# Both heads of a pair at once in grouped-query and neighbourhood attention

## The chip, the cores and the metric

The kernel runs on one core of a Trainium2 chip. The metric is the device time of one execution in microseconds; of several runs the median is given. A core has TensorE (PE in the profile; its weight loads stand apart as PEld), VectorE (DVE), ScalarE (ACT), GpSimd (POOL) and SyncE (SP), each with its own instruction queue, worked through in order. They meet at semaphores. Matmul results go to PSUM, eight banks of 128 partitions by 512 f32; all else is in SBUF.

## The reference

Two models in series on 512 tokens of width 1024. The first has a recurrent mixer, a feed-forward layer, stick-breaking attention with 16 heads and a second feed-forward layer. The change lies in the second model, whose core is:

```python
def second_block(x, mem, w_in, b_gate, na_rpb, gqa_q_gain, gqa_k_gain, w_mem_kv, w_branch, ...):
    z = jnp.einsum('bsd,df->bsf', x, w_in[l])
    q_na, k_na, v_na, q_g, k_g, v_g, q_m, gate_logits = jnp.split(z, _split_points(), axis=-1)
    y_na = neighbourhood_attention(...)      # 8 heads of 64
...
    y_gqa = gqa_attention(...)               # 8 query heads of 64, 2 key heads
...
    y_mem = memory_attention(...)            # 4 heads of 128
    branches = jnp.stack([y_na, y_gqa, y_mem], axis=2)
    proj = jnp.einsum('bsgk,gkd->bsgd', branches, w_branch[l])
    gates = jax.nn.sigmoid(gate_logits + b_gate[l]).reshape(B, S, N_BRANCH, D)
    merged = jnp.sum(gates * proj, axis=2)
    mix = jnp.einsum('bsd,de->bse', merged, w_out[l])
    x = layer_norm(DN_ALPHA * x + mix, ln1_g[l], ln1_b[l])
    ffn = expert_choice_ffn(x, w_router[l], w_gate_up[l], w_down[l])
    return layer_norm(DN_ALPHA * x + ffn, ln2_g[l], ln2_b[l])

def gqa_attention(...):                      # q, k: rms_norm, then rope
    s = jnp.einsum('bkgqd,bskd->bkgqs', qi, k) * scale
    p = jax.nn.softmax(s, axis=-1)
    return jnp.einsum('bkgqs,bskd->bqkgd', p, v)

def neighbourhood_attention(...):            # 8 rows x 64 columns; 4 blocks of 16 query columns
    scores = jnp.einsum('rcqhd,rckwhd->hrcqkw', qg, k_blk) * (1.0 / math.sqrt(dh))
    scores = jnp.where(in_win, scores + bias, NEG_INF)
    p = jax.nn.softmax(scores, axis=(-2, -1))
    out = jnp.einsum('hrcqkw,rckwhd->rcqhd', p, v_blk)
```

In grouped-query attention four query heads share one key head. In neighbourhood attention a query sees all 8 rows and 16 columns; `bias` comes from a table with 15 x 31 entries for each head, and entries outside the window are masked.

## The kernel before

Activations are held transposed: features on partitions, the 512 tokens along the free axis. A dense product in f32 is made of three matmuls (lines 1604 to 1606): high half by high half, low by high, high by low. `HH`/`HL` (and `YP` for attention outputs) are the halves of the activations, `WH`/`WL` those of the weights. SP loads weights into six `RAW` buffers; ACT makes `WH` (L958) and DVE `WL` (L1206), in three buffers each. A "unit" of weights is up to eight 128 x 128 tiles, and a "triple" the three matmuls of one tile.

**Order.** `Order` writes the program as a list of steps. `claim` takes the PSUM bank that was released longest ago, and notes the event after which it may be written; `release` gives it back with that event. Every engine's program walks the same list and issues its part of each step, so the order of the list is the order on each engine. The second mixer has banks 0 to 5 for this ring and banks 6 and 7 for attention outputs. Its order is written by hand in `mixer2_order`.

**Weave.** `staged` goes over the units of an attention. Per unit it adds the score step, then takes pieces of other work from the generator `work` (the "fill"; `counts` says how many pieces), then adds the value step that has become due, then the turn of the unit two places back. A piece is four triples: twelve matmuls. "Turn" is the transposing of a probability tile: PE multiplies it by the identity (L1647) into a bank, ACT copies it to SBUF (L969).

**Grouped-query stage.** Heads are treated in four pairs `c`. The two heads of a pair lie on partitions 0 to 63 and 64 to 127 of `ZG` (queries) and `KG` (keys, both key heads), which are views of the tile `AT`. A unit is one head and 128 queries: 32 units. Its score is one matmul with 64 contracted rows (L1782). DVE takes the maximum from the bank (L1225) and scales it (L1227), ACT makes the exponential and its sum (L964) into one of three `PG`, DVE takes the reciprocal (L1232) and scales `PG` (L1234), PE turns it, and ACT copies into `GT2`. When a head's four units are turned, its values are made by four matmuls over 512 columns (L1797). The fill is the gates and branch products of the memory attention (group 2), and the queries of pairs 1 to 3 with norm and rope: one product in plain f32 for the norm, one for the rotation (L1775), a reciprocal over 512 columns (L1432). The program lists f32 matmuls as two passes (`x2` in the timeline for one instruction).

**First neighbourhood pair.** After the last values, `finish(pairs[0]["qkv"]())` projects the queries, keys and values of pair 0 with nothing woven in.

**Neighbourhood stage.** A unit is one head and one block of 16 query columns in all 8 rows: 128 queries, 32 units. `nq` stores the queries ordered by column block. The score matmul has 256 keys, the band of 32 columns in 8 rows (L1807). The bias is added by a second matmul into the same bank (L1811): `anti`, a matrix that reverses the order of partitions, times a window of `BI`. `BI` holds the table's rows as POOL's queue loads them (L909, 16 small DMAs for a pair); in that layout the queries run backwards. DVE adds the mask and takes the maximum in one instruction into `SN`; ACT makes the exponential into `PN`, DVE scales, PE turns (two transposes), ACT copies into `NT`, and two matmuls over 128 columns make the values (L1828). The fill is the projection of pairs 1 to 3 and the gates and branches of the grouped-query output (group 1); their gate products are added up by POOL (L913).

## Time and profile before

| | us |
|---|---|
| median of 3 runs | 2364.69 (2362.87 to 2369.45) |
| the profiled execution | 2363.75 |
| its span in the trace | 2362.0 |
| busy in the span: PE, DVE | 2197.8 (93%), 1113.5 (47%) |
| busy in the span: ACT, POOL | 720.3 (30%), 156.4 (7%) |

The memory attention and all that goes before it end at 1302.76 in the trace, when the first grouped-query score begins. The grouped-query stage lasts until 1466.29; its last fill matmul begins at 1420.08. The first neighbourhood pair is projected until 1485.50, and the last neighbourhood values begin at 1674.44. Behind them come the group-0 branches, the output product, a layer norm, the router and the experts. In a timeline equal instructions in a row are one line with `xN`, and its second number is from the start of the first to the end of the last; matmuls overlap, so that the next line can begin before this one ends.

### The profile page before, as it was taken

What the parts mean: (1) busy time and instruction counts of PE and PEld (TensorE: products, weight loads), DVE (VectorE), ACT (ScalarE), POOL (GpSimd) and SP (SyncE); (2) the same over time, 40 slices, a digit from 0 to 9 for tenths busy, and PEclk for the clock granted to TensorE, in tenths of its full rate; (3) what the DMA queues carried; (4) which work ended last, traced back from release to release, by engine and by line L of the source; (5) the groups of instructions that cost most, each with busy time, mean ns of one, the idle gap of its engine ahead of it and who ended that gap; (6) DMA issues with size and microseconds to landing.
All of it is one profiled execution on the core that took longest, in us unless ns stands there. A gap on an engine that the chain in (4) does not pass through costs nothing.

```text
span 2362.0 us, 24184 instructions
## 1 busy us (share of the span) xinstructions
PE 2197.8 (93%) x9722; PEld 1523.0 (64%) x9722; DVE 1113.5 (47%) x1602; ACT 720.3 (30%) x1051; POOL 156.4 (7%) x159
## 2 busy tenths in 40 slices
PE   6989999999999899999989998999995899999995
PEld 4768888888777788888877554777783433334331
DVE  7876443445665654344566554444455211111114
ACT  2553322333555432222344443233333000000002
POOL 2221000001000100000100001210002000000001
PEclk9989999999999999999999999999998899999997
DMA  4222223223111222332341111321226799999992
GB/s 160 89 71 99 96 75 124 90 74 123 63 56 61 81 90 85 112 99 80 108 134 49 50 50 33 76 56 54 81 72 249 282 371 406 410 409 411 410 418 85
DMA packets 83662, 350.74 MB, mean 148 GB/s; under 512 B 9152, under 2 KB 10832, under 8 KB 66912
## 3 DMA queue, kind: packets, MB, share of 16 engines
q1 hardware_dynamic: 80448, 342.92, 39.5%
q0 software_dynamic: 2240, 2.71, 0.8%
q10 hardware_dynamic: 864, 3.57, 0.4%
q8 instruction: 78, 1.28, 0.2%
q14 instruction: 32, 0.26, 0.0%
HBM read 347.06 MB, written 2.10 MB: 148 GB/s over the span
## 4 chain that ended last, share of the span: by engine, by line
PE 85%; DVE 8%; ACT 3%; issue 3%; POOL 0%; DMA 0%; ACTq 0%; DVEq 0%; POOLq 0%
PE PS L1604 19%; PE PS L1606 18%; PE PS L1605 18%; PE PS L1904 10%; PE PS L1935 5%; PE PS L1947 2%; PE PS L1647 2%; PE PS L1887 2%; PE PS L1797 1%; PE PS L1782 1%; PE PS L1811 1%; PE PS L1807 1%; PE PS L1703 1%; PE PS L1828 1%; PE PS L1717 1%
## 5 line engine op out<-in xcount | busy, mean ns | idle before, releaser
L1604 PE MATMUL PS<-HH,WH 128*128 128x512 f32 x1392 | 564.8, 406 | 33.7 <-DVE HL L1210 20.7
L1606 PE MATMUL PS<-HH,WL 128*128 128x512 f32 x1392 | 547.3, 393 | 0.0
L1605 PE MATMUL PS<-HL,WH 128*128 128x512 f32 x1392 | 547.0, 393 | 0.0
L1206 DVE TENSOR_TENSOR WL<-RAW,WH 128x1024 fp32r<-128x1024 f32 (+5 forms) x300 | 339.7, 1132 | 245.0 <-ACT WH L958 243.7
L958 ACT ACTIVATE WH<-RAW 128x1024 fp32r<-128x1024 f32 (+4 forms) x278 | 263.3, 948 | 311.3 <-PE PS L1606 311.3
L1604 PEld LDWEIGHTS PS<-HH,WH 128*128 128x128 f32 x1392 | 264.3, 190 | 107.4 <-issue 28.1
L1606 PEld LDWEIGHTS PS<-HH,WL 128*128 128x128 f32 x1392 | 264.2, 190 | 57.0
L1605 PEld LDWEIGHTS PS<-HL,WH 128*128 128x128 f32 x1392 | 264.9, 190 | 55.2 <-issue 2.4
L1904 PE MATMUL PS<-SL,XS 128*64 128x512 f32 x952 | 227.2, 595 | 0.0
L1313 DVE TENSOR_TENSOR X<-X,PS 128x512 f32<-128x512 f32 x116 | 79.6, 686 | 228.4 <-PE PS L1947 162.2
L1904 PEld LDWEIGHTS PS<-SL,XS 128*64 128x64 f32 x952 | 70.1, 137 | 133.8 <-issue 126.8
L1604 PE MATMUL PS<-MH,WH 128*128 128x512 f32 x352 | 136.9, 389 | 0.0
L1605 PE MATMUL PS<-ML,WH 128*128 128x512 f32 x352 | 136.9, 389 | 0.0
L1606 PE MATMUL PS<-MH,WL 128*128 128x512 f32 x352 | 136.9, 389 | 0.0
L1935 PE MATMUL PS<-SL,HT 128*64 128x512 f32 x480 | 113.3, 602 | 5.5 <-ACT HT L969 5.5
L1180 ACT ACTIVATE SG<-PS 128x512 f32<-128x512 f32 x16 | 8.7, 594 | 328.7 <-PE PS L1904 328.7
L1935 PEld LDWEIGHTS PS<-SL,HT 128*64 128x64 f32 x480 | 36.3, 138 | 77.3 <-issue 69.8
L1216 DVE TENSOR_TENSOR U<-PS,RS 128x512 f32<-128x512 f32 x44 | 30.4, 691 | 107.2 <-PE PS L1606 107.2
L1606 PEld LDWEIGHTS PS<-MH,WL 128*128 128x128 f32 x352 | 66.1, 188 | 13.8
L1604 PEld LDWEIGHTS PS<-MH,WH 128*128 128x128 f32 x352 | 66.1, 188 | 13.7
L1605 PEld LDWEIGHTS PS<-ML,WH 128*128 128x128 f32 x352 | 66.1, 188 | 13.6
L1579 DVE TENSOR_TENSOR SG<-SG,PS 128x512 f32<-128x512 f32 x16 | 10.3, 684 | 132.3 <-ACT SG L1180 132.3
(281 smaller groups left out, 2744.4 us busy)
## 6 DMA issues: line engine op xcount, KB each, us to landing
SL<-in_wgu_dram SPq DMA_DIRECT2D x119, 1024.0 KB, 11.7
SL<-in_wdn_dram SPq DMA_DIRECT2D x60, 1024.0 KB, 9.7
RAW<-in_w_dram SPq DMA_DIRECT2D x46, 512.0 KB, 3.3
RAW<-in_wg_dram SPq DMA_DIRECT2D x44, 512.0 KB, 3.3
RAW<-in_wu_dram SPq DMA_DIRECT2D x44, 512.0 KB, 3.3
RAW<-in_wd_dram SPq DMA_DIRECT2D x32, 384.0 KB, 3.1
RAW<-in_wqkv_dram SPq DMA_DIRECT2D x24, 512.0 KB, 3.3
RAW<-in_wd_dram SPq DMA_DIRECT2D x32, 320.0 KB, 2.9
```

What stands on the lines that cost most here:

```text
L958: e.activation(WH[u % NSPL][:, 0:n], RAW[u % NRAW][:, 0:n], ACT.Copy).then_inc(*whs.did("u", u))
L1206: e.tensor_tensor(wl, raw, wh.bitcast(F), ALU.subtract).then_inc(*wlo.did("u", u))
L1216: e.tensor_tensor(dst, src, r, ALU.mult).then_inc(*scaled.did(*event))
L1313: e.tensor_tensor(X[:, c, :], X[:, c, :], bank(*key), ALU.add).then_inc(*xup.did(*key))
L1604: e.matmul(out, wh[:, w], xh, start=k == 0, stop=False)
L1605: e.matmul(out, wh[:, w], xl, start=False, stop=False)
L1606: m = e.matmul(out, wl[:, w], xh, start=False, stop=k == g.total - 1)
L1647: m = e.transpose(bank(*key)[:, 128 * j:128 * j + 128], src, ident)
L1887: m = e.matmul(bank("ga", q, d)[:, 0:256], P[:, tc, 128 * d:128 * d + 128], PE[:, tc, :], start=tc == 0 and P is XNH, stop=tc == 3 and P i ...
L1904: m = e.matmul(bank("h", i, n)[64 * e2:64 * e2 + 64, :], XS[z][:, k, x0:x0 + 64], SL[(l0 + e2) % NSLOT][:, 512 * n:512 * n + 512], start=k ...
L1935: m = e.matmul(bank("y", i, n)[64 * e2:64 * e2 + 64, :], HT[:, 2 * k + f, 64 * e2:64 * e2 + 64], SL[(l0 + e2) % NSLOT][:, 1024 * f + 512 * ...
L1947: e.matmul(bank("sc", i, d), SG[:, 128 * d:128 * d + 128], GT[i % 2][:, :], start=True, stop=True).then_inc(*ex.did("sc", i, d))
```

## The change

- **Units of two heads.** In both stages a unit is now a pair of heads and 128 queries: 16 units each. The scores of the two heads are issued one behind the other on array rows 0 to 63 and 64 to 127, into a bank each. The values are issued in turns on array columns 0 to 63 and 64 to 127. In the grouped-query stage they are made after every unit, 128 columns wide, in place of once per head, 512 wide. `PG` and `GT2` have four buffers.
- **Softmax.** Two maxima, one small scaling, two exponentials, one small reciprocal, two scalings. The turn of a unit is eight transposes (four in the neighbourhood stage) and two copies by ACT (one).
- **Bias.** The bias matmul goes. POOL adds bias and mask of both heads into `BM` in a new step `na_mask`, 16 in all; the queries are written backwards (`by_column`) so that they fit `BI`, and the outputs are read backwards again. The mask constant is reversed once, at the start of the mixer, by two plain f32 matmuls with `anti` of 512 and 256 columns and two copies by DVE. DVE adds the scores to `BM` in place and takes the maximum.
- **Weave.** The turn comes one unit behind the score, not two. Pieces of fill are two triples, six matmuls; `counts` is [4, 3] and [5]. Pair 0's projection is part of the grouped-query fill. The banks of a unit's two scores come free with its exponentials (with DVE's pass in the neighbourhood stage).

The core of the diff, with its new line numbers in the order further down (1604 has become 1674, 1606 1676, 1647 1717, 1782 1860, 1797 1878, 1807 1888, 1828 1906):

```diff
 def mixer2_order(o):
+    o.claim("mask")
+    o.claim("mask2")
     o.add("m2_consts")
+    for n in range(2):
+        o.release((("mask",), ("mask2",))[n], "gated", "mask", n)
...
+    def staged(groups, work, counts, lag=2):
         units = [(g, u) for g in groups for u in range(g["n"])]
         then = None
-        for i in range(len(units) + 2):
+        for i in range(len(units) + lag):
             if i < len(units):
                 g, u = units[i]
                 while u == 0 and not g["there"]():
...
             if then:
                 then()
             then = None
-            if i >= 2:
-                g, u = units[i - 2]
-                then = g["turn"](u, (i - 2) % 3)
+            if i >= lag:
+                g, u = units[i - lag]
+                then = g["turn"](u, (i - lag) % 3)
+        if then and lag == 1:
+            step(work)
+            then()
+            then = None
...
+            for y in range(2):
+                o.claim("gs", c, u, y)
+            o.add("gqa_score", c, u)
+            for y in range(2):
+                o.release(("gs", c, u, y), "prob", "gs", c, u, y)
         def turn(u, k):
-            key = ("gt2", c, u)
-            o.claim(*key)
-            o.add("gqa_turn", c, u, k)
-            o.release(key, "turn", *key)
+            for y in range(2):
+                o.claim("gt2", c, u, y)
+            o.add("gqa_turn", c, u)
+            for y in range(2):
+                o.release(("gt2", c, u, y), "turn", "gt2", c, u, y)
             def values():
-                if u // 4 == 0:
+                if u == 0:
                     claim_out("go", c)
-                o.add("gqa_values", c, u // 4)
-                if u // 4 == 1:
+                o.add("gqa_values", c, u)
+                if u == 3:
                     release_out(("go", c), "lo", "b", 4 + c)
-            return values if u % 4 == 3 else None
-
-        return {"n": 8, "there": lambda: f"q{c}" in there, "score": score, "turn": turn}
-
...
-    staged([gqa_pair(c) for c in range(4)], gqa_work(), [1])
+            return values
+
+        return {"n": 4, "there": lambda: f"q{c}" in there, "score": score, "turn": turn}
...
+                yield from o.lin_steps((name, c), [("w2", (4 * i + c,), 8)], "h", done, size=2)
+                if i == 1 and c == 0:
+                    o.add("na_bias", 0)
+                    o.add("na_mask", 0, 0)
+            yield
+            for j in range(2):
+                natural(("nvn", c, j))
             there.add(("na", c))
...
+            o.add("na_turn", c, u)
+            o.release(("nt", c, u), "turn", "nt", c, u)
+            if c < 3:
+                o.add("na_mask", c + 1, u)
+            if (c, u) == (0, 3):
+                o.add("na_bias", 3)
...
+    na_pairs = [na_pair(c) for c in range(4)]
+
+    def gqa_work():
+        br = branches(2, 2)
         for c in range(1, 4):
-            q = pairs[c]["qkv"]()
-            for w in "qqbbbqqqqq":
-                step(q if w == "q" else br, 1)
+            q = rope(f"q{c}", 12 + c, 2)
+            for w in "qqqqbbqbbbbqbb" if c == 1 else "qqqqbbqbbbbqbbbbbb":
+                step(q if w == "q" else br)
                 yield
         yield from br
-
-    o.add("na_start")
-    finish(pairs[0]["qkv"]())
-    staged(pairs, na_work(), [1, 2, 1])
+        yield from na_pairs[0]["qkv"]()
+
+    def na_work():
+        br = branches(1, 2)
+        for c in range(1, 4):
+            q = na_pairs[c]["qkv"]()
+            for w in "qqqqqqqqqqqqbbbbqqbbbbbbbb":
+                step(q if w == "q" else br)
+                yield
+        yield from br
+
+    staged([gqa_pair(c) for c in range(4)], gqa_work(), [4, 3], 1)
+    o.add("na_bias", 1)
+    for u in range(1, 4):
+        o.add("na_mask", 0, u)
+    o.add("na_bias", 2)
+    staged(na_pairs, na_work(), [5], 1)
...
-        PG = [sb(f"PG{i}", [128, T], F, pg) for i in range(3)]
-        GT2 = [sb(f"GT2{i}", [128, 4, T], F, pg) for i in range(2)]
+        PG = [sb(f"PG{i}", [128, T], F, pg) for i in range(4)]
+        GT2 = [sb(f"GT2{i}", [128, 4, 128], F, pg) for i in range(4)]
...
+        NT = [t[:, :].rearrange("p (j n) -> p j n", n=128) for t in (ST, SA)]
...
+        def by_column(t):
+            return t.rearrange("p (c n) -> p c n", c=4)[:, :, ::-1].rearrange("p c (r i) -> p r c i", i=16)
...
+                elif kind == "na_mask":
+                    c, cb = a
+                    f = BAND[cb] - 16 * cb + 16
+                    if c:
+                        e.wait_ge(*tr("nt", c - 1, cb))
+                    elif cb == 1:
+                        e.wait_ge(*att("go", 3, 3))
+                    if cb == 0:
+                        e.wait_ge(*gated("mask", 1))
+                        e.wait_ge(*d_bias[c % 2](c, 1, 7))
+                    m = cst("mask", 256 * (0, 1, 1, 2)[cb], 256).rearrange("p (a w) -> p a w", a=8)
+                    e.tensor_tensor(BM[cb][:, :, :].rearrange("p y (a w) -> p y a w", a=8),
+                                    BI[c % 2][:, :, :].rearrange("p y (a w) -> p y a w", a=8)[:, :, :, f:f + 32],
+                                    m.unsqueeze(1).to_broadcast([128, 2, 8, 32]), ALU.add).then_inc(
+                        *pool.did("bm", c, cb))
...
-                    dve_softmax_max(e, key, bank(*key), k, 0.125)
-                    dve_softmax_div(e, key, PG[k][:, :], k)
+                    c, u = a
+                    k = 8 * (u % 2)
+                    for y in range(2):
+                        if y == 0:
+                            e.wait_ge(*att("gs", c, u))
+                        e.tensor_reduce(SM[:, k + y:k + y + 1], bank("gs", c, u, y), AX.X, ALU.max).then_inc(
+                            *masked.did("gs", c, u, y))
+                    e.wait_ge(*masked("gs", c, u, 1))
+                    e.tensor_scalar(SM[:, k + 2:k + 4], SM[:, k:k + 2], -0.125, None, ALU.mult).then_inc(
+                        *smax.did("m", "gs", c, u))
+                    e.wait_ge(*prob("gs", c, u, 1))
+                    e.reciprocal(SM[:, k + 6:k + 8], SM[:, k + 4:k + 6]).then_inc(*smax.did("r", "gs", c, u))
+                    e.wait_ge(*smax("r", "gs", c, u))
+                    for y in range(2):
+                        P = PG[2 * (u % 2) + y][:, :]
+                        e.tensor_scalar(P, P, SM[:, k + 6 + y:k + 7 + y], None, ALU.mult).then_inc(
+                            *smax.did("p", "gs", c, u, y))
...
-                    e.tensor_tensor_reduce(SN[k][:, :], bank(*key)[:, 0:256], cst("mask", 256 * (0, 1, 1, 2)[u % 4], 256),
-                                           1.0, -3e38, ALU.add, ALU.max, SM[:, 4 * k:4 * k + 1]).then_inc(*masked.did(*key))
-                    dve_softmax_max(e, key, None, k, 1.0)
-                    dve_softmax_div(e, key, PN[k][:, :], k)
+                    c, u = a
+                    k = 8 * (u % 2)
+                    e.wait_ge(*att("ns", c, u))
+                    e.wait_ge(*pool("bm", c, u))
+                    for y in range(2):
+                        S2 = BM[u][:, y, :]
+                        e.tensor_tensor_reduce(S2, bank("ns", c, u, y)[:, 0:256], S2, 1.0, -3e38, ALU.add, ALU.max,
+                                               SM[:, k + y:k + y + 1]).then_inc(*masked.did("ns", c, u, y))
...
+                elif kind == "m2_consts":
+                    for n, (a0, w) in enumerate(((0, 512), (512, 256))):
+                        if o.before[(("mask",), ("mask2",))[n]]:
+                            e.wait_ge(*freed(("mask", "mask2")[n]))
+                        e.matmul(bank(("mask", "mask2")[n])[:, 0:w], anti, cst("mask", a0, w), start=True,
+                                 stop=True).then_inc(*red.did("mask", n))
...
-                    e.matmul(bank("gs", c, u), ZG[c % 2][p:p + 64, 128 * qc:128 * qc + 128], KG[p:p + 64, :], start=True,
-                             stop=True).then_inc(*att.did("gs", c, u))
+                    for y in range(2):
+                        p = 64 * y
+                        m = e.matmul(bank("gs", c, u, y), ZG[c % 2][p:p + 64, 128 * u:128 * u + 128], KG[p:p + 64, :],
+                                     start=True, stop=True)
+                    m.then_inc(*att.did("gs", c, u))
...
+                    e.wait_ge(*turn("gt2", c, u, 1))
                     for j in range(4):
-                        m = e.matmul(bank("go", c)[p:p + 64, :], VG[:, 128 * j + p:128 * j + p + 64], GT2[y][:, j, :],
-                                     start=j == 0, stop=j == 3)
-                    m.then_inc(*att.did("go", c, y))
+                        for y in range(2):
+                            p = 64 * y
+                            m = e.matmul(bank("go", c)[p:p + 64, 128 * u:128 * u + 128], VG[:, 128 * j + p:128 * j + p + 64],
+                                         GT2[2 * (u % 2) + y][:, j, :], start=j == 0, stop=j == 3, skip_group_check=True)
+                    m.then_inc(*att.did("go", c, u))
...
-                    e.matmul(out, NQ[c % 2][p:p + 64, 0, 128 * cb:128 * cb + 128],
-                             NQ[c % 2][p:p + 64, 1, :].rearrange("p (r w) -> p r w", r=8)[:, :, bs:bs + 32], start=True,
-                             stop=False)
-                    e.wait_ge(*d_bias[c % 2](c, 1, 7))
-                    e.matmul(out, anti, BI[c % 2][:, y, :].rearrange("p (a w) -> p a w", a=8)[:, :, f:f + 32], start=False,
-                             stop=True).then_inc(*att.did("ns", c, u))
+                    for y in range(2):
+                        p = 64 * y
+                        m = e.matmul(bank("ns", c, u, y)[:, 0:256], NQ[c % 2][p:p + 64, 0, 128 * u:128 * u + 128],
+                                     window(u, NQ[c % 2][p:p + 64, 1, :]), start=True, stop=True)
+                    m.then_inc(*att.did("ns", c, u))
```

TensorE in the first half of the grouped-query stage, from the end of one run of fill to the next. The kernel before:

```order
L1606 MATMUL PS<-HH,WL 128x512
L1797 MATMUL PS<-GT,AT 64x512 x4
L1647 MATMUL PS<-C,PG 128x128 x4
L1782 MATMUL PS<-AT 128x512
L1604 MATMUL PS<-HH,WH 128x512
```

The changed kernel, the same place:

```order
L1676 MATMUL PS<-HH,WL 128x512
L1878 MATMUL PS<-GT,AT 64x128 x8
L1717 MATMUL PS<-C,PG 128x128 x8
L1860 MATMUL PS<-AT 128x512 x2
L1674 MATMUL PS<-HH,WH 128x512
```

One head's four value matmuls over 512 columns, which came once in four units, have become eight over 128 columns in every unit, and the one score two.

TensorE in the neighbourhood stage, a unit between two runs of fill. The kernel before:

```order
L1606 MATMUL PS<-HH,WL 128x512
L1828 MATMUL PS<-NT,NV 64x128 x2
L1647 MATMUL PS<-C,PN 128x128 x2
L1807 MATMUL PS<-AT 128x256
L1811 MATMUL PS<-BI,C 128x256
L1604 MATMUL PS<-HH,WH 128x512
```

The changed kernel:

```order
L1676 MATMUL PS<-HH,WL 128x512
L1906 MATMUL PS<-ST,NV 64x128 x4
L1717 MATMUL PS<-C,BM 128x128 x4
L1888 MATMUL PS<-AT 128x256 x2
L1674 MATMUL PS<-HH,WH 128x512
```

The matmul with `BI` is gone, and the rest stands twice in a unit, of which there are half as many.

DVE in the grouped-query stage, one softmax and the fill behind it. The kernel before:

```order
L1225 TENSOR_REDUCE SM<-PS 128x1
L1227 TENSOR_SCALAR SM<-SM 128x1
L1232 RECIPROCAL SM<-SM 128x1
L1234 TENSOR_SCALAR PG<-PG,SM 128x512
L1432 RECIPROCAL ST<-ST 128x512
L1434 SCALAR_TENSOR_TENSOR AT<-AT,V,ST 128x512
L1206 TENSOR_TENSOR WL<-RAW,WH 128x512
L1403 SCALAR_TENSOR_TENSOR ACC<-ACC,PS 128x512
```

The changed kernel:

```order
L1504 TENSOR_REDUCE SM<-PS 128x1 x2
L1507 TENSOR_SCALAR SM<-SM 128x2
L1510 RECIPROCAL SM<-SM 128x2
L1514 TENSOR_SCALAR PG<-PG,SM 128x512 x2
L1256 TENSOR_TENSOR WL<-RAW,WH 128x512
L1456 SCALAR_TENSOR_TENSOR ACC<-ACC,PS 128x512
L1485 RECIPROCAL ST<-ST 128x512
L1487 SCALAR_TENSOR_TENSOR AT<-AT,V,ST 128x512
```

The chain of both heads stands in one block ahead of the fill's work, and the rope's long reciprocal one place further on.

## Rows read from the trace of the kernel before

**Rows 1.** The page, chain of work that ended last: shares of the span by engine.
```profile
PE 85%; DVE 8%; ACT 3%; issue 3%; POOL 0%; DMA 0%; ACTq 0%; DVEq 0%; POOLq 0%
```
**Rows 2.** Windows view: us, busy (instructions) by engine, PEclk, DMA share, GB/s.
```profile
1302.76:1466.29 163.53, 154.00 (x534) 83.43 (x533) 90.29 (x177) 69.58 (x131) 0.00 (x0) 0.97 0.13 42
1466.29:1485.50 19.21, 17.61 (x81) 14.29 (x81) 7.50 (x11) 3.67 (x4) 16.71 (x32) 1.00 0.61 109
1485.50:1674.44 188.94, 188.41 (x850) 135.71 (x849) 86.41 (x230) 58.33 (x132) 27.79 (x40) 1.00 0.21 60
```
**Rows 3.** Timeline of PE, grouped-query stage: start, duration, instruction, [idle before <-releaser].
```profile
1352.85 1.12 PE L1782 MATMUL PS<-AT 64*128 64x512 f32 x2
1353.90 0.50 PE L1604 MATMUL PS<-YP,WH 128*128 128x512 f32 x1
...
1356.86 3.65 PE L1797 MATMUL PS<-GT,AT 128*64 128x512 f32 x8
1360.44 0.66 PE L1647 MATMUL PS<-C,PG 128*128 128x128 f32 x4
```
**Rows 4.** Timeline of PE, neighbourhood stage, one unit and the fill behind it.
```profile
1527.89 0.65 PE L1828 MATMUL PS<-NT,NV 128*64 128x128 f32 x4
1528.47 0.44 PE L1647 MATMUL PS<-C,PN 128*128 128x128 f32 x2
1528.84 0.70 PE L1807 MATMUL PS<-AT 64*128 64x256 f32 x2
1529.47 0.70 PE L1811 MATMUL PS<-BI,C 128*128 128x256 f32 x2
1529.82 0.58 PE L1604 MATMUL PS<-HH,WH 128*128 128x512 f32 x1
1530.24 0.39 PE L1605 MATMUL PS<-HL,WH 128*128 128x512 f32 x1
...
1532.53 0.39 PE L1606 MATMUL PS<-HH,WL 128*128 128x512 f32 x1
1532.85 0.32 PE L1828 MATMUL PS<-NT,NV 128*64 128x128 f32 x1
```
**Rows 5.** PE's groups by form; the last row is of 1466.29 to 1674.43.
```profile
L1797 PE MATMUL PS<-GT,AT 128*64 128x512 f32 x64 | 34.0, 681 | 7.0 <-ACT GT L969 7.0
L1604 PE MATMUL PS<-HH,WH 128*128 128x512 f32 x56 | 24.1, 430 | 0.0
...
L1604 PE MATMUL PS<-HH,WH 128*128 128x512 f32 x160 | 67.5, 422 | 0.0
```
**Rows 6.** Timeline of PE near the end of the grouped-query stage.
```profile
1436.09 5.34 PE L1797 MATMUL PS<-GT,AT 128*64 128x512 f32 x8 [2.16 <-ACT GT L969]
```
**Rows 7.** Timeline of PE in the first model's attention, two heads at once.
```profile
762.77 2.43 PE L1703 MATMUL PS<-QK 64*128 64x384 f32 x16
...
765.68 2.37 PE L1727 MATMUL PS<-WT,VN 128*64 128x512 f32 x16
```
**Rows 8.** Timeline of DVE in the bare end of the grouped-query stage.
```profile
1431.43 0.68 DVE L1225 TENSOR_REDUCE SM<-PS 128x1 f32<-128x512 f32 x1
1432.15 0.15 DVE L1227 TENSOR_SCALAR SM<-SM 128x1 f32<-128x1 f32 x1
1433.21 0.16 DVE L1232 RECIPROCAL SM<-SM 128x1 f32<-128x1 f32 x1 [0.91 <-ACT PG L964]
1433.41 0.48 DVE L1234 TENSOR_SCALAR PG<-PG,SM 128x512 f32<-128x512 f32 x1
```
**Rows 9.** DVE's groups by form in the grouped-query stage.
```profile
L1432 DVE RECIPROCAL ST<-ST 128x512 f32<-128x512 f32 x3 | 10.1, 3353 | 3.9 <-ACT ST L1101 3.9
```
**Rows 10.** Timeline of POOL in the neighbourhood stage.
```profile
1524.61 8.33 POOL L909 DMA_DIRECT2D BI<-in_rpb_dram  x16 [17.30 <-PE PS L1811]
1547.19 1.28 POOL L913 TENSOR_TENSOR ACC<-ACC,GX 128x512 f32<-128x512 f32 x1 [14.25 <-DVE GX L1403]
```
**Rows 11.** Timeline of PE at the start of the second mixer.
```profile
1201.92 0.55 PE L1604 MATMUL PS<-YP,WH 128*128 128x256 f32 x1 [5.14 <-DVE YP L1210]
```

247 lines of the change are left out of this document (117 added, 130 removed).

## The prediction

> **What bounds the kernel now.** I read the chain of waits first: TensorE makes up 85% of it [rows 1]. A saving therefore counts only if it takes away TensorE's time or its idling. I then split the second mixer into stretches [rows 2]. From the first grouped-query score at 1302.76 us to the last neighbourhood value matmul at 1674.44 us there are 371.7 us: 163.5 for the grouped-query stage, 19.2 in which the first neighbourhood pair is projected with nothing else running, and 188.9 for the neighbourhood stage. DVE is busy for 90.3, 7.5 and 86.4 us of them, so no other engine is the limit there yet.
>
> Durations of single matmuls mislead, since they overlap; I price by the distance from one start to the next. The dense matmuls that are woven in (the "fill") start 0.229 us apart (ten steps from 1530.24 to 1532.53), and a run of 12 takes 3.03 us in the neighbourhood stage and 2.96 in the grouped-query stage (1353.90 to 1356.86), so a run costs 0.28 and 0.21 on top of its 12 x 0.229 [rows 3, 4]. One head's score, with 64 contracted rows, takes 1.05, a head's four value matmuls over 512 columns 3.58 for eight passes (1356.86 to 1360.44), 0.43 a pass [rows 3]. In the neighbourhood stage one head's quarter costs values 0.58, two transposes 0.37, score 0.63, bias 0.35, together 1.93, and there are 32 [rows 4]. A narrow pass (128 columns) more costs (0.58 - 0.37) / 2, about 0.11.
>
> The end of the grouped-query stage differs. Its fill is used up at 1420, and the last 10 scores and 13 turns run bare. The value groups wait 7.0 us in all for ACT's copies [rows 5], and the one at 1436.09 takes 5.34 us behind its wait, where 3.65 is usual [rows 3, 6]; two later ones do the same. The granted clock over the stage is 0.97, against 1.00 in the stretches behind it [rows 2]: after these pauses the engine ran for a while at the lower of its two levels, 1.2 instead of 2.4 GHz. Waits and slow passes are worth some 7.0 + 3 x 1.6 = 12 us.
>
> **The change, part by part.** The fill itself doesn't change: 56 + 32 triples in the first stretch and 160 + 32 in the rest [rows 5]; the 32 are the branch matmuls, as the code has them, 840 matmuls in all; the new order has 336 + 504. I price the new stretch afresh and compare it with 371.7.
>
> *Both heads at once.* Do two halves of the array overlap? The first model's attention already issues its heads so. L1703 has 1280 columns of scores per head, for two heads, in two passes; L1727 the same number of value columns, on column halves. At 0.43 us per 512-column pass, one head alone would take 2560 / 512 x 0.43 = 2.15, two in turn 4.3. Measured are 2.43 and 2.37 [rows 7]: they overlap nearly fully, on row halves and on column halves. So a pair's score costs 1.05 as one head's did: 16 x 1.05 = 16.8. A unit's values are eight matmuls over 128 columns; four such passes take 0.58, so eight overlapped steps take 0.58 + 4 x 0.11 = 1.02: 16.3. Eight transposes behind values take 0.37 + 6 x 0.11, 1.02: 16.3. The six rope matmuls have two passes of 0.43: 5.2. Together 54.6.
>
> *Neighbourhood stage.* The bias matmul is gone. A unit now has values 0.58 (four overlapped steps), four transposes 0.59, and a score pair of 0.35 (as L1811, which stood last before fill): 1.52, 16 times 24.3, and 4 x 8 x 0.11 = 3.5 for the NB transposes: 27.8.
>
> *Fill.* 840 x 0.229 = 192.4; 18 runs x 0.21 and 19 x 0.28 add 9.1, where 22 and 34 runs added 14.1. Together 201.5.
>
> Sum: 201.5 + 54.6 + 27.8 = 283.9 without waits.
>
> *Waits that take their place.* A unit's score now needs banks that the exponentials of the unit before it read, so there is a loop: score, two maxima, two exponentials, next score. In the bare stretch one head's chain on DVE is 0.72 from the maximum's start to the next step, 1.06 to the reciprocal, 0.20 to the scaling and 0.48 for that [rows 8]; the other head adds a maximum (0.68), an exponential (about 0.8, what the 1.06 holds besides the 0.15 step and the hops) and a scaling (0.4, overlapped): 4.3 us, in which DVE stands still for ACT. From score to next score the loop needs 0.1 + 0.72 + 0.68 + 1.06 + 0.8 + 1.1 = 4.5, and TensorE has work for 5.5 to 8.8 between them. What matters is DVE's backlog. Over the first twelve units DVE has 12 x 4.3 = 51.6 plus fill work: 34 operations over 512 columns at 0.68, 6 over 1024 at twice that and 3 reciprocals of 3.35 [rows 8, 9], 41.4, in all 93.0. TensorE has 93.9 (228 fill matmuls 52.2, entries 2.5, ropes 5.2, 12 scores 12.6, 11 turns 11.2, 10 value groups 10.2). They are level. One place walked through: behind unit 2's chain DVE has four pieces of fill, and behind unit 1's the rope's reciprocal, so unit 3's maxima start about 3.3 us after its score; its interval of 6.8 us (12 fill matmuls, rope, values, turn, score) is then 1.0 short. There are three such places: 3 us. At the end of the stage the last values wait for two copies right behind the turn: 0.9. At the end of the neighbourhood stage two value groups wait for a copy each: 1.5. 1.0 for everything else. Together 6.4; bounds 0 and 25 (first rival).
>
> *Moved to POOL.* 16 adds of bias and mask, at 1.27 each as L913 over the same size [rows 10], take the place of the bias matmuls. Only the first pair is tight: behind the last grouped-query values POOL issues 16 DMAs (8.33) and then adds, so BM1 is ready 9.7 us later; its score comes after 1.0 + 0.35 + 7.2, DVE then waits about 1 us, and two runs of fill (14 us) lie before the transposes that need it. With that cover gone it would cost 1 us. Four adds and 16 issues in a pair, 13.4 us, lie beside 37 us of TensorE.
>
> *Mask reversal.* Two f32 matmuls of 512 and 256 columns at the start of the mixer, two passes each, 0.86 + 0.43 and 0.2 for entering. The chain to ScalarE, the reciprocal and the YP split, for which TensorE waits 5.14 us [rows 11], starts behind them. So they cost 1.5 in full; the two DVE copies fall into a time in which DVE waits for that chain.
>
> **Result.** 283.9 + 6.4 = 290.3 against 371.7 is -81.4; with +1.5, -79.9. The profiled execution took 2363.75 us (span 2362.0), so 2283.9; the runs' median is 0.9 above it: **2285 us**. What follows (last branches, experts) is the same in both orders and only moves earlier.
>
> **The rivals.**
> - *DVE becomes the bound of the grouped-query stage* (0.22). For it: 93.0 against 93.9 us leave nothing for hops or late gates. Against: the last four units have slack, and back to back operations start closer than their durations. If each of 16 units loses 1 to 1.3 us more: +16 to +21, 2301 to 2306. The Trainium skill (TensorEngine Tiling (Array Packing), PSUM Bottleneck) warns that packing speeds up TensorE but not the emptying of PSUM, which may become the limit; by that rule the time would be this rival's.
> - *The halves don't overlap in narrow passes* (0.08), or the change doesn't do what it says. Weight loads come four times as often per column as in the widest part of L1727. Values would cost 16 x 0.87 + 16 x 0.44 = 21 more: 2306; scores too, 13.8 + 6.9 more: 2327. Against: L1727's narrow part is inside its 2.37.
> - *No new waits, and the mask reversal hidden* (0.12): 2277.
> - *Slower than before* (0.02): POOL's adds read a broadcast mask and windows of the bias tile, a form that no row shows. A pair leaves POOL 37 us, of which 8.3 go to issues and 3.4 to the gate adds; above 6.4 us an add, POOL sets the pace. To lose 87 us over the 12 adds of the last three pairs each would need 13.7 us, eleven times its row: 2372 and more.
>
> **Chances.** Forecast (2280 to 2292) 0.55, the rivals as above, 0.01 for anything else. The range 2273 to 2306 holds the forecast, the case without waits and most of the DVE case. About 0.3% (7 us) is what a measurement of this kernel can tell from no change; all but the last rival lie far beyond: faster 0.97, same 0.01, slower 0.02.
>
> **What would show it.** Matmuls of L1860 and of L1878 starting in pairs, 1.05 us a score pair and 1.02 a value group. A granted clock of 1.00 over the whole stretch. TensorE waiting about 1 us ahead of L1860 at three places, not at sixteen. The stretch at 290 us. POOL's adds at 1.3 us, and DVE waiting for them once. The forecast is wrong if score pairs take 2 us, if TensorE waits ahead of most scores, or if stretches outside this one move by more than 2 us.

## The result and the profile after

The changed kernel takes 2297.84 us in the median of 4 runs (2295.93 to 2298.65), the kernel before 2364.44; the ratio is 0.9714, with a 95% interval of 0.9697 to 0.9730. The forecast was 2285. It is faster by 66.6 us, 12.8 less than forecast. That is inside the range of 2273 to 2306, above the forecast's own band (2280 to 2292, chance 0.55), and below the band of the first rival (2301 to 2306). The profiled execution took 2297.08 us, its span is 2295.3.

The page of the changed kernel, shares of its chain by engine (before: [rows 1]):

```profile
PE 82%; DVE 10%; ACT 4%; issue 3%; POOL 0%; DMA 0%; ACTq 0%; DVEq 0%; POOLq 0%
```

The two stages of the changed kernel in the windows view (columns as in [rows 2]): from the first grouped-query score to the first neighbourhood score, with the projection of neighbourhood pair 0 inside, and from there to the end of the last values.

```profile
1306.19:1455.12 148.93, 138.59 (x805) 97.56 (x805) 90.23 (x155) 71.54 (x135) 10.33 (x19) 0.99 0.21 58
1455.12:1606.30 151.18, 149.69 (x786) 114.12 (x785) 81.94 (x199) 55.56 (x116) 60.38 (x70) 1.00 0.31 78
```

Together 300.1 us stand against the 371.7 of [rows 2]: -71.6. In the second stage TensorE is busy for all but 1.5 us. In the first it isn't: 10.3 us are idle. TensorE's waits in that stage, by what ended them (us in total, times, longest):

```profile
PE PS L1860 <- DVE AT L1497: 5.2, 3, 3.4
PE PS L1674 <- DVE ACC L1456: 2.8, 3, 1.3
PE PS L1845 <- ACT SQ L1140: 1.2, 1, 1.2
PE PS L1878 <- ACT GT L1012: 0.8, 1, 0.8
PE PS L1851 <- DVE ACC L1456: 0.4, 1, 0.4
```

L1860 is the score, L1497 VectorE's last step of the rope of a pair's queries, L1456 VectorE's addition of a branch product, whose bank the fill wants next. TensorE's timeline in that stage, one unit (against [rows 3]):

```profile
1359.99 1.09 PE L1878 MATMUL PS<-GT,AT 128*64 128x128 f32 x16
1361.01 1.09 PE L1717 MATMUL PS<-C,PG 128*128 128x128 f32 x8
1362.04 1.13 PE L1860 MATMUL PS<-AT 64*128 64x512 f32 x4
1363.10 1.12 PE L1851 MATMUL PS<-AT,C 128*128 128x512 f32 x2
1365.50 0.47 PE L1674 MATMUL PS<-HH,WH 128*128 128x512 f32 x1 [1.28 <-DVE ACC L1456]
```

From start to start the values of both heads take 1.02 us, their eight transposes 1.03, both scores 1.06: within 0.01 of the forecast's 1.02, 1.02 and 1.05. The halves overlap: the first passes of the two heads start 0.01 us apart in both groups. The last row is one of the waits. The timeline of a neighbourhood unit (against [rows 4]):

```profile
1584.03 0.66 PE L1906 MATMUL PS<-SA,NV 128*64 128x128 f32 x8
1584.62 0.66 PE L1717 MATMUL PS<-C,BM 128*128 128x128 f32 x4
1585.20 0.70 PE L1888 MATMUL PS<-AT 64*128 64x256 f32 x4
1585.83 0.50 PE L1674 MATMUL PS<-HH,WH 128*128 128x512 f32 x1
```

Values 0.59 and turn 0.58 are as forecast; the score pair takes 0.63, where 0.35 was put. The longest pause, where the rotation of pair 3's queries stands right ahead of that pair's first score:

```profile
1406.11 1.02 PE L1851 MATMUL PS<-AT,C 128*128 128x512 f32 x2
1410.56 1.82 PE L1860 MATMUL PS<-AT 64*128 64x512 f32 x4 [3.43 <-DVE AT L1497]
1412.32 0.79 PE L1674 MATMUL PS<-HH,WH 128*128 128x512 f32 x1
1412.91 0.63 PE L1675 MATMUL PS<-HL,WH 128*128 128x512 f32 x1
```

Behind 3.43 us of idleness the score pair takes 1.76 us from start to start, where 1.06 is usual, and a fill matmul 0.43 (1412.91 to the next at 1413.34), where 0.23 is. These are passes at the lower clock level (1.2 GHz where 2.4 is usual; the granted clock is the third number from the end of the row, 0.54), 1.6 us in all with the run of fill behind the score (6.58 for 24 matmuls against 5.66):

```profile
1410.56:1414.19 3.63, 3.63 (x8) 1.79 (x9) 1.46 (x3) 0.23 (x1) 0.00 (x0) 0.54 0.01 2
```

### The profile page after: what moved, and what is told of

It reads as the page before. It is cut to its first block, busy times and chain, and to the rows that moved or that the text cites. A ratio compares the mean times of both kernels' runs of the same rounds, so it can differ in the third digit from the quotient of the medians.

```text
span 2295.3 us, 24304 instructions
## 1 busy us (share of the span) xinstructions
PE 2132.7 (93%) x9854; PEld 1506.7 (66%) x9854; DVE 1102.7 (48%) x1540; ACT 715.8 (31%) x1035; POOL 182.7 (8%) x175
## 4 chain that ended last, share of the span: by engine, by line
PE 82%; DVE 10%; ACT 4%; issue 3%; POOL 0%; DMA 0%; ACTq 0%; DVEq 0%; POOLq 0%
PE PS L1674 19%; PE PS L1676 18%; PE PS L1675 18%; PE PS L1982 10%; PE PS L2013 5%; PE PS L2025 2%; PE PS L1965 2%; PE PS L1717 2%; PE PS L1779 1%; DVE XC L1322 1%; PE PS L1793 1%; PE PS L1803 1%; DVE X L1565 1%; PE PS L1860 1%; DVE WL L1256 1%
## 5 line engine op out<-in xcount | busy, mean ns | idle before, releaser
L1649 DVE TENSOR_TENSOR SG<-SG,PS 128x512 f32<-128x512 f32 x16 | 10.3, 683 | 132.3 <-ACT SG L1230 132.3
```

## The experiments

Each is an edit of the changed kernel, run once (the last two four times), and is judged by its stage lengths in the trace. "The stage" is the grouped-query stage, from the first grouped-query score to the first neighbourhood score: 148.9 us in the changed kernel. Stage lengths are finer than the whole time, since identical code scatters outside the edited stages, above all ahead of the mixer: from the first matmul to the mixer's norm the changed kernel and the nine edits with the same code there take 1176.3 to 1182.3 us. Stage lengths scatter too, but only by the clock. Of the three edits that leave the grouped-query stage as it is, two have 148.9 us and one 150.2, with the same waits (10.3 us) and with passes at the lower clock for 5.9 us behind the wait of 3.42 where the changed kernel has 3.6. So a difference of 1.3 us in that stage can be the clock alone. The neighbourhood stage has 151.2 us in every run that leaves it as it is. Three theories stood against each other for the 12 us lost in the grouped-query stage: the place of the rope (1), VectorE's load (2), and a few tight places where both meet (3).

**Rope of pair 3 earlier.**

```diff
-            for w in "qqqqbbqbbbbqbb" if c == 1 else "qqqqbbqbbbbqbbbbbb":
+            for w in "qqqqbbqbbbbqbb" if c < 3 else "qqqqbbqbbbbqbbbbbb":
```

> One edit to the changed kernel: four branch pieces behind the queries of pair 2 are moved behind those of pair 3, so that the last rotation of pair 3 stands two pieces of fill ahead of pair 3's first score, as it does for pairs 1 and 2, and not right ahead of it. Theory 1 (the waits come from where the rope stands): the wait of 3.43 us ahead of that score becomes about 0.9 as at pairs 1 and 2, and the slow passes behind it (0.7 at the score, 0.9 at the fill) go: stage 148.9 us becomes about 144.8, time about 2293.7. Theory 2 (VectorE's whole load sets the pace): the wait only changes its place, under 1 us is gained, 2297.

Measured 2302.06 us; the stage became longer, 154.0 us. The 3.43 us went, and another wait came in its place. ScalarE's timeline there:

```profile
1378.55 0.20 ACT L1153 ACTIVATION_READ_ACCUMULATOR PG<-PS,SM 128x1 f32 x1
1387.59 1.06 ACT L1001 ACTIVATE WH<-RAW 128x1024 fp32r<-128x1024 f32 x1 [8.84 <-PE PS L1676]
1390.54 0.63 ACT L1140 ACTIVATE SQ<-AT 128x512 f32<-128x512 f32 x1 [1.89 <-DVE AT L1266]
1391.08 1.06 ACT L1012 ACTIVATE GT<-PS 128x512 f32<-128x512 f32 x2
```

ScalarE stood 8.84 us at a weight split. The queries of pair 3 now began in the middle of a gate's unit of weights; the split wants the buffer of that unit, which TensorE only gave back after the queries. The rope's square, the copies and the exponentials were queued behind it, and TensorE waited 3.8 us for the square. Neither theory 1 nor theory 2 had this wait. At the stage's end, 3.2 us came from fill that was left over: one piece more behind the last values, and a wait of 1.6 for the neighbourhood values.

**Softmax split on VectorE.**

```diff
             if i < len(units):
...
                 g["score"](u, i % 3)
-            step(work, counts[i % len(counts)])
+            n = counts[i % len(counts)]
+            if i < len(units) and "div" in g:
+                step(work)
+                n -= 1
+                units[i][0]["div"](units[i][1])
+            step(work, n)
...
                 elif kind == "gqa_score":
...
+                elif kind == "gqa_div":
+                    c, u = a
+                    k = 8 * (u % 2)
                     e.wait_ge(*prob("gs", c, u, 1))
```

> One edit to the changed kernel: on VectorE the reciprocal and the two scalings of a unit stand behind the first piece of fill after its score, not straight behind the maxima, in both stages; in the changed kernel VectorE stands still for 1.51 us there in each of 16 units, waiting for ScalarE's exponentials (24.2 us in the grouped-query stage). Theory 2 (VectorE's load with its standing is the limit): the fill's waits for banks of branch products (2.8 + 0.4 us), and two of the three waits for roped queries (0.87, 0.89) go; the third (3.43) shrinks by 1.5: -5 to -6, time about 2292. Theory 1 (place of the rope alone): the waits for roped queries shrink by under 1 us each, time 2296 to 2297.

Measured 2302.65 us, of which 4.1 more than in the changed kernel lie among the experts, in code that the edit doesn't touch. The stage: 147.6 us, -1.4. TensorE's waits there fell by 2.5 us: those ahead of the first scores of pairs 1 and 2 went, as theory 2 had it, but the third is still 3.0, and the fill's waits for banks of branch products grew (4.0 us, from 3.2). Passes at the lower clock took about 1.2 us more than in the changed kernel. The neighbourhood stage, where the edit applies too, has 151.2 us as before. VectorE's waits in the grouped-query stage show why so little was gained:

```profile
DVE WL L1263 <- ACT WH L1008: 23.9, 13, 2.5
...
DVE SM L1520 <- ACT PG L1160: 8.2, 6, 1.5
```

In the changed kernel the second wait is 24.2 us, 16 times, and the first 7.6. Much of the wait has only changed its name: the weight split that VectorE now reaches needs ScalarE's half, which stands behind the same exponentials on ScalarE.

**Mask reversed in the table of constants.**

```diff
-        c[:, CST["mask"] + 256 * n:CST["mask"] + 256 * n + 256] = np.where(m, 0.0, -1e30)
+        c[:, CST["mask"] + 256 * n:CST["mask"] + 256 * n + 256] = np.where(m, 0.0, -1e30)[::-1]
```

with the two matmuls, the two copies and POOL's wait on them taken out.

> One edit to the changed kernel: the mask stands reversed in the table of constants, and the two matmuls and two VectorE copies that reverse it at the start of the second mixer go. Measured between the two traces, TensorE is 1.3 us later there. If that is the whole price: the norm's first matmul comes 1.3 us sooner, time 2296.5. If the reversal also cost the 0.9 us by which the memory attention starts later still: 2295.6. If it was hidden (a rival of the prediction): no change, 2297.8.

Measured 2292.86 us, 4.2 less than the changed kernel's profiled execution, 3.8 of it ahead of the mixer's norm, where the scatter is larger than the mask's price. So whole times don't give that price; the changed kernel's trace does, from the start of the first row to that of the second:

```profile
1186.06 1.45 PE L1756 MATMUL PS<-C 128*128 128x512 f32 x4
1187.16 0.58 PE L1674 MATMUL PS<-HH,WH 128*128 128x512 f32 x1
```

1.1 us, and 0.19 for the next matmul's late start behind it (0.42 against 0.23): 1.3. The wait for the norm's split is 5.1 us with and without the reversal, so nothing hid it. The 0.9 us by which the memory attention started later are 0.7 less in five of the nine experiments that have the reversal: most of them come and go, and aren't its price.

**Projection of neighbourhood pair 0 outside the weave.**

```diff
-        yield from na_pairs[0]["qkv"]()
...
+    finish(na_pairs[0]["qkv"]())
     o.add("na_bias", 1)
```

> One part of the change undone: the projection of neighbourhood pair 0 is no part of the grouped-query fill, but runs with nothing woven in behind that stage, as before. The fill is then 240 matmuls and is used up after about ten of sixteen units. If the weave carries gain: each of the six bare units has 3.1 us of TensorE's work in a loop of at least 4.5, about +8; the bare projection waits 1.6 as before, and slow passes come behind the waits, 1 to 4: +11 to +14, time 2309 to 2312. If the gain comes from the overlap of the heads alone: +0 to +3, up to 2301.

Measured 2298.83 us. The stage, with the bare projection in it, has 153.4, +4.5. The mechanism was right and the count wrong: the fill lasts for 14 of the 16 units, not ten. Only two scores stand bare. The end of the stage, with the value groups waiting for copies:

```profile
1428.61 1.13 PE L1860 MATMUL PS<-AT 64*128 64x512 f32 x4
1430.91 1.09 PE L1878 MATMUL PS<-GT,AT 128*64 128x128 f32 x16 [1.17 <-ACT GT L1012]
1431.93 1.09 PE L1717 MATMUL PS<-C,PG 128*128 128x128 f32 x8
1434.90 1.09 PE L1878 MATMUL PS<-GT,AT 128*64 128x128 f32 x16 [1.88 <-ACT GT L1012]
```

So the new place of this projection is worth 4.5 of the 71.6 us.

**Rope earlier, unit of weights whole.**

```diff
-            for w in "qqqqbbqbbbbqbb" if c == 1 else "qqqqbbqbbbbqbbbbbb":
+            for w in ("qqqqbbqbbbbqbb", "qqqqbbqbbbbq", "qqqqbbqbbbbqbbbbbb")[c - 1]:
```

> The edit of the first experiment again, but the queries of pair 3 now start at the end of a whole branch product (six pieces moved, not four). In the first experiment they started in the middle of a gate's unit of weights; ScalarE's next split then waited 8.8 us for a weight buffer, with the rope's square and the exponentials queued behind it. Theory 3 (place of the rope, if no unit of weights is left half used): the wait of 3.43 us and the slow passes behind it go, about 0.9 is left, and the wait for a weight buffer is under 2: stage (first grouped-query score to first neighbourhood score) 148.9 becomes 144.5 to 145.5. Theory 2 (VectorE's load): the stage gains under 1 us, 148 or more.

Measured 2293.77 us, but the stage has 148.9 us as before. ScalarE's wait for a weight buffer fell to 2.1 and the 3.43 went. Not all pausing did: the last score of pair 2 now starts after 1.74 us of idleness, for which the profile names no cause, and passes at the lower clock stand behind it (granted clock 0.58 and 0.50 in the next two stretches of 1.8 us):

```profile
1397.03 1.85 PE L1860 MATMUL PS<-AT 64*128 64x512 f32 x4 [1.74 <-issue]
```

Up to the last values 3.2 us were gained, and the same 3.2 lost at the end, by the fill that is left over as in the first experiment. A gain and a loss of different causes: this run alone can't decide for theory 3.

**Maxima taken twice, and a short reciprocal.**

```diff
+                        e.tensor_reduce(SM[:, 16 + k // 2 + y:17 + k // 2 + y], bank("gs", c, u, y), AX.X, ALU.max)
                         e.tensor_reduce(SM[:, k + y:k + y + 1], bank("gs", c, u, y), AX.X, ALU.max).then_inc(
                             *masked.did("gs", c, u, y))
```

> The changed kernel with VectorE's two maxima of every grouped-query unit taken twice (the extra result goes to an unused place): 1.2 us more of VectorE in each of 16 units, 19 in all. Theory 2 (VectorE's load sets this stage's pace, the prediction's first rival): +13 to +19, stage 162 to 168. Theory 3 (only the seven places at which rope or branch work meets a softmax are tight): each of them grows by up to 1.2, the rest is hidden: +5 to +8, stage 154 to 157.

```diff
-                    e.reciprocal(ST[:, :], ST[:, :]).then_inc(*roped.did("r", name))
+                    w = 512 if name in ("k", "q0") else 8
+                    e.reciprocal(ST[:, 0:w], ST[:, 0:w]).then_inc(*roped.did("r", name))
```

> The changed kernel with the rope's reciprocal of the queries of pairs 1 to 3 done over 8 columns and not 512, so that these queries are scaled otherwise than in the reference: VectorE has 3.25 us less at each of three places. Theory 3: the maxima behind it start sooner, the wait for pair 3's queries goes from 3.43 to about 0.2 to 1, the 0.70 and 1.28 us waits of the fill and the 0.87 and 0.89 at pairs 1 and 2 shrink: -4 to -7, stage 142 to 145. If the chain over ScalarE and TensorE is what takes the time and not VectorE's queue: under -1.

Measured 2302.21 and 2287.92 us. The stage in the windows view, first with the maxima twice, then with the short reciprocal (VectorE's busy time is the third in the row, 109.18 and 81.24):

```profile
1301.05:1461.78 160.73, 141.00 (x805) 99.04 (x804) 109.18 (x187) 70.89 (x135) 10.55 (x19) 0.97 0.18 54
```

```profile
1301.50:1445.27 143.77, 138.08 (x805) 98.22 (x804) 81.24 (x155) 71.90 (x135) 10.44 (x19) 0.99 0.21 60
```

With 19.0 us more on VectorE the stage is 11.8 longer, with 9.0 less it is 5.2 shorter: 0.6 us for each. Theory 2 wanted 13 or more and theory 3 at most 8; it lies between. TensorE's waits become 19.6 and 5.7 us (10.4 in the changed kernel), for the most part at the same places; with the maxima twice a wait of 1.45 ahead of another score comes in, one that waits for exponentials. In waits alone it is 9.2 more and 4.7 less, 0.5 us for each microsecond of VectorE. VectorE is no full bound and has no slack either: it is busy for 90.2 us, stands 24.2 for the exponentials and 7.6 for weight splits, 122 of 149.

**Values head by head.**

```diff
-                    for j in range(4):
-                        for y in range(2):
+                    for y in range(2):
+                        for j in range(4):
```

> The changed kernel with the eight grouped-query value matmuls of a unit issued head by head (four of one head, then four of the other), not in turns. If the two column halves overlap only because neighbours in the queue lie on different halves: a unit's values take 0.58 + 12 x 0.11 = 1.9 us, not 1.03, 16 x 0.87 = +14, stage 163. If the order doesn't matter (what is saved is saved by the narrower write alone): values stay at 1.03, no change.

Measured 2297.49 us. The value group in TensorE's timeline:

```profile
1323.36 1.58 PE L1878 MATMUL PS<-GT,AT 128*64 128x128 f32 x16
1324.88 1.09 PE L1717 MATMUL PS<-C,PG 128*128 128x128 f32 x8
```

1.52 us against 1.02: the order in turns matters, for 0.5 us a unit and not 0.87. Within the group the first and the last four passes start singly, 0.11 us apart, and the eight in the middle overlap, two in each 0.11. The other thing it shows is larger. TensorE works 16 x 0.5 = 8 us more, and the stage has 151.0 us, only 2.0 more; the waits fell from 10.4 to 6.2 and the slow passes went (granted clock 1.00). So of the 8 us that the order in turns saves TensorE, three quarters come back as idling and slow passes in the changed kernel.

**A bias matmul back on TensorE.**

```diff
-                                     window(u, NQ[c % 2][p:p + 64, 1, :]), start=True, stop=True)
+                                     window(u, NQ[c % 2][p:p + 64, 1, :]), start=True, stop=False)
+                    for y in range(2):
+                        m = e.matmul(bank("ns", c, u, y)[:, 0:256], anti, cst("cos", 0, 256), start=False, stop=True)
```

> The changed kernel with two matmuls of the old bias matmul's shape (the reversing matrix by 256 columns of a constant, one for each head's bank) put behind every pair of neighbourhood scores; the values they add are not the bias, so the output differs, POOL's adds stay. This prices the part 'bias off TensorE'. As the prediction has it (0.35 us of TensorE for each head and quarter, nothing hiding it): +9 to +11.2, the neighbourhood stage 151.0 becomes 160 to 162. If TensorE's time is given back there as waits (VectorE or POOL sets the pace in this stage): under +4.

Measured 2307.16 us; the neighbourhood stage has 164.6, +13.4. TensorE's timeline:

```profile
1488.78 0.70 PE L1888 MATMUL PS<-AT 64*128 64x256 f32 x4
1489.41 1.13 PE L1891 MATMUL PS<-C 128*128 128x256 f32 x4
1490.19 0.58 PE L1674 MATMUL PS<-HH,WH 128*128 128x512 f32 x1
```

0.78 us a unit, 12.5 in all, and 0.05 more for each run of fill behind it. In this stage TensorE's time counts in full.

**POOL's adds four times over.**

```diff
+                    e.tensor_tensor(BM[cb][:, :, :].rearrange("p y (a w) -> p y a w", a=8),
+                                    BI[c % 2][:, :, :].rearrange("p y (a w) -> p y a w", a=8)[:, :, :, f:f + 32],
+                                    m.unsqueeze(1).to_broadcast([128, 2, 8, 32]), ALU.add).then_inc(
+                        *pool.did("bm0", c, cb))
+                    e.wait_ge(*pool("bm0", c, cb))
...
```

> The changed kernel with each of POOL's 16 adds of bias and mask made four times over, one behind the other, with the same result: about 5.2 us for 1.28. This tests the prediction's rival that is slower than before, in which POOL sets the pace from 6.4 us an add. If that bound holds: the adds are late only at the first pair, where VectorE waits for them with the split of the weights queued behind it; +0 to +4, neighbourhood stage 151 to 155. If POOL's time is passed on from the first microsecond: 15 x 3.9 = +58.

Measured 2298.70 us, neighbourhood stage 153.8, +2.6, with POOL busy for 125.5 us of it (60.4 in the changed kernel). One split of weights behind VectorE's wait is late:

```profile
DVE BM L1559 <- POOL BM L964: 13.8, 3, 6.9
```

```profile
PE PS L1689 <- DVE WL L1271: 2.3, 1, 2.3
```

The first row is of VectorE's waits, the second of TensorE's. POOL has room for adds of 5.2 us at a price of 2.6 us, as the rival's bound of 6.4 said; where the bound lies was not tried.

**Both edits, with the fill spread over the stage.** With the mask of the third experiment:

```diff
-            for w in "qqqqbbqbbbbqbb" if c == 1 else "qqqqbbqbbbbqbbbbbb":
+            for w in ("qqqqbbqbbbbqbb", "qqqqbbqbbbbqbbbb", "qqqqbbqbbbbqbbbbbb")[c - 1]:
...
-    staged([gqa_pair(c) for c in range(4)], gqa_work(), [4, 3], 1)
+    staged([gqa_pair(c) for c in range(4)], gqa_work(), [4, 4, 3, 4, 3, 4, 4, 3], 1)
```

> The changed kernel with two edits that the earlier experiments point to. The mask stands reversed in the table of constants. The grouped-query weave has pieces per unit 4,4,3,4,3,4,4,3, not 4,3, and the queries of pair 3 start after five branch units, at the end of a unit of weights, so that each pair's last rotation stands two or three pieces ahead of its first score, no unit of weights is left half used, and the fill still ends with the stage. Theory 3 (place): the wait of 3.43 and the slow passes go and nothing takes their place: grouped-query stage 148.9 becomes 143.5 to 145.5; with 1.3 for the mask, about 6 us under the changed kernel, 2291.5 in the median. If VectorE's load alone decides (theory 2), the stage stays at 147 or more: 2295 or more.

Measured 2290.17 us in the median of 4 runs (ratio to the kernel before 0.9686, 0.9671 to 0.9700). The stage has 144.7 us, -4.3, inside theory 3's range and under theory 2's 147. No score waits for the rope any more, and the tail of 3.2 is gone. TensorE's waits are 6.0 us, and passes at the lower clock stand behind the longest, 2.4 us. The stage, and half of the waits:

```profile
1303.08:1447.76 144.68, 138.49 (x805) 98.21 (x804) 89.84 (x155) 71.38 (x135) 10.51 (x19) 0.99 0.20 60
PE PS L1667 <- DVE ACC L1449: 3.1, 2, 2.4
```

**VectorE relieved on top of it.** With the split of the second experiment:

```diff
+                elif kind == "gqa_score":
+                    c, u = a
+                    k = 8 * (u % 2)
+                    e.wait_ge(*smax("r", "gs", c, u))
+                    P = PG[2 * (u % 2) + 1][:, :]
+                    e.tensor_scalar(P, P, SM[:, k + 7:k + 8], None, ALU.mult).then_inc(*pool.did("p", "gs", c, u, 1))
...
-                    for y in range(2):
-                        P = PG[2 * (u % 2) + y][:, :]
-                        e.tensor_scalar(P, P, SM[:, k + 6 + y:k + 7 + y], None, ALU.mult).then_inc(
-                            *smax.did("p", "gs", c, u, y))
+                    P = PG[2 * (u % 2)][:, :]
+                    e.tensor_scalar(P, P, SM[:, k + 6:k + 7], None, ALU.mult).then_inc(
+                        *smax.did("p", "gs", c, u, 0))
```

> The kernel of the experiment before with VectorE relieved: the second head's scaling by the reciprocal (0.44 us, 16 times) is done by POOL, which has nothing to do in this stage, and VectorE takes the first piece of fill between the maxima and the reciprocals (edit of the second experiment, worth 1.4 alone). From the two runs that changed VectorE's work (19.2 us more cost 11.8; 9.8 less gave 5.2: 0.53 to 0.61 us a us), 7 us less should give 3.7 to 4.3, and the second edit 1.4: stage 138 to 140.5, time about 2286 to 2287. If the load no longer matters once rope work is well placed: as the experiment before, within 1.

Measured 2281.41 us in the median of 4 runs (2280.77 to 2284.47), ratio to the kernel before 0.9655 (0.9639 to 0.9671), and 16.4 us under the changed kernel's median. The stage and TensorE's waits in it:

```profile
1300.17:1438.58 138.41, 136.44 (x806) 97.06 (x805) 83.73 (x139) 71.36 (x135) 38.14 (x32) 1.00 0.22 63
```

```profile
PE PS L1685 <- DVE ACC L1462: 1.2, 2, 0.6
PE PS L1883 <- ACT GT L1021: 0.8, 1, 0.8
```

10.5 us less than in the changed kernel and 6.3 less than in the run before, inside the range that the slope gave: VectorE's load counts also with the rope well placed. 2.0 us of waits are left, and the clock is at 1.00. POOL's scaling takes 1.86 us where VectorE's takes 0.49, in an engine that is otherwise busy for about 10 us there. Of the 16.3 us between the two profiled executions 10.5 are the stage's and 1.3 the mask's; the other 4.5 lie ahead of the mixer's norm, in code that is the same, and no edit explains them.

## Why the prediction was right, and where it was off

The direction and the mechanism held: both heads cost what one did. The forecast's own band did not: the profiled execution came 13.2 us above the 2283.9, and the stretch took 300.1 us where 290 was to show, with a granted clock of 0.99 in its first stage where 1.00 was. The wide range holds it because it was drawn to take in most of the VectorE rival. The 13.2 us are made up so.

- **TensorE's work.** Forecast 283.9 us without waits, measured 300.1 - 11.8 of waits - 1.6 of slow passes = 286.7. Grouped-query scores, values and turns were right to 0.01 us each, and fill took about what was forecast. The term that was mis-sized is the neighbourhood score pair: 0.35 was taken from L1811's row, because that one stood last before fill, but what counts is that the half-array score stands there now, and its own row has 0.63 [rows 4]. 16 x 0.28 = 4.5 us, of which a shorter entry into fill gives about 2 back (30 matmuls in 7.04 us: 0.17 above 30 x 0.229, where 0.28 was put, 19 times). A bias pair on the full array ahead of the same fill took 0.78 us, or 0.39 a matmul. The Trainium skill (TensorEngine Tiling (Array Packing), Key Properties) states that a change of the tiling mode drains TensorE, which would fit a half-array matmul that costs more ahead of fill than its passes; no run here isolates it.
- **Waits.** Forecast 6.4 us, measured 11.8, and 1.6 of slow passes behind the longest; this is the larger miss, 7.0. Three waits ahead of scores were forecast, about 1 us each, and there are three: 0.87, 0.89 and 3.43. But the step failed in what they wait for. The forecast looked at banks that the exponentials hold; the scores wait for their queries' rope. That two of the three had the size forecast was luck. The walk-through took VectorE's work for one place and never asked how many pieces lie between the last rotation and the score that needs it: two at pairs 1 and 2, none at pair 3. The fill's waits for banks of branch products (2.8 us) and that for the rope's square (1.2) were not in the sum either, beyond the 1.0 "for everything else". The waits at the ends of the two stages were right: 0.8 us (forecast 0.9) and 1.5 (1.5).
- **The rival of VectorE as the bound** had +16 to +21 by a loss in each of 16 units; the stage's waits stand at nine places. A microsecond of VectorE's work is worth 0.6 by the maxima taken twice and the short reciprocal. It is half true: VectorE's backlog doesn't set the pace in every unit, but where a piece is late TensorE has nothing else to do. The rule of the Trainium skill (TensorEngine Tiling (Array Packing), PSUM Bottleneck) that the emptying of PSUM may become the limit is borne out in part: in the grouped-query stage, where the fill waits 3.2 us for banks that VectorE empties, though more (6.4 us) goes to waits for the rope; and not in the neighbourhood stage, where adding 0.78 us of TensorE's work to each of 16 units cost 13.4 us, all of it.
- **Bias and mask to POOL, the reversal.** The price of a bias matmul was about right (0.39 a head, forecast 0.35). Adds took 1.28 to 2.28 us, VectorE waited once, 1.3 us. The rival in which POOL sets the pace was rightly small. The reversal cost 1.3, forecast 1.5.
- **Elsewhere.** The forecast had 0 for the other stretches; they are 3.5 us longer in this execution. The prediction counted itself wrong on this point from 2 us; but identical code scatters by 6 us ahead of the norm, so that bound was too tight for a single execution, and the 3.5 can't be put down to the change or cleared of it.

As a sum: 2283.9 + (286.7 - 283.9) + (13.4 - 6.4) - 0.2 + 3.5 = 2297.0.

Placing the rope, keeping weight units whole and spreading the fill gave back 4.3 us of the stage; taking 6 us from VectorE (89.8 to 83.7 us busy), and splitting its softmax, another 6.3. That leaves 2.0 of the 10.4 us of waits, and no slow passes. So the idle time of that stage was lost to the order and the amount of VectorE's and ScalarE's work. TensorE's own work accounts for 2.8 us of the miss.

## What to carry to other kernels

When an edit makes the bounding engine faster, count for each of its steps what its input's chain needs and how many pieces of other work stand between producer and consumer; the share that comes back as idling is decided there. Of 8 us it was three quarters in one stage, and of 13 us none in the next. Pieces that are woven must not cut through a unit whose buffer someone else waits for, and fill should run out with the stage. Test how much an engine is the limit by adding and removing a known amount of its work: the slope tells more than its busy share.

## What the runs showed of the hardware

- Two heads on column halves take 1.02 us in turns and 1.52 head by head, for the same 16 passes. Head by head it is still less than the 1.9 that single steps of 0.11 us give, since the eight passes in the middle overlap in twos.
- After 3.43 us of idleness TensorE ran at the lower clock for 3.6 us, with fill matmuls 0.43 us apart and not 0.23; after waits up to 1.3 us no slow passes followed in the changed kernel. The length of the wait alone doesn't tell: in the experiments slow passes came behind 1.74 us (granted clock 0.58), 2.20 (0.63) and 2.40 (0.63), and none behind 2.34 and 2.42 (1.00). Nor does it tell how long they last: behind 3.42 us, in code that is the same, it was 5.9 us at 0.50. In the run with the maxima twice, waits of 19.6 us left a granted clock of 0.97.
- POOL's scaling of 128x512 by a column took 1.86 us (VectorE's 0.49), an add of bias and mask over windows and a broadcast mask 1.28, at times 2.28.
